# Second input projection as three float32r products by column group and half depth, with the embedding norm in two VectorE operations and the meta rows first

## The reference, cut to what matters

```python
x = x + (1.0 + gate[:, None, :]) * y            # end of the first block
x = rmsnorm(x, final_g)
...
meta = jnp.broadcast_to(meta_tokens...)         # 16 meta rows in front
h = _layernorm(jnp.concatenate([meta, x], axis=1), ln_emb_g, ln_emb_b)   # 528 rows
...
z = jnp.einsum('bld,dc->blc', h, w_in)          # [528,1024] x [1024,1472]
q_a, kv_a, k_pe, q_g, k_g, v_g = jnp.split(z, IN_OFFSETS, axis=-1)
# rmsnorm of parts of z, rotations, attention over 528 keys, w_o, layernorm,
# router, 32 experts with 4 per token, layernorm
```

## Time and profile before

| | |
|---|---|
| median of 3 runs | 2195.67 us (2194.2 to 2202.55) |
| profiled execution, its own time | 2200.66 us |
| its span in the trace | 2198.9 us |
| mean granted TensorE clock | 0.966 of full |
| PE busy | 2063.0 us (94%) |
| DVE busy | 1729.9 us (79%) |
| ACT busy | 1298.4 us (59%) |
| POOL busy | 289.6 us (13%) |

### The profile page before, as it was taken

The page is one execution under the profiler, slowest core; times in us unless marked ns, Lnnn a source line. Parts: engine busy times, 40 slices in busy tenths (PEclk is TensorE's granted clock), DMA queues, the critical chain, the costliest instruction groups (busy, mean ns, idle before and its releaser), DMA issues.

```text
span 2198.9 us, 28821 instructions
## 1 busy us (share of the span) xinstructions
PE 2063.0 (94%) x8636; PEld 1508.0 (69%) x8636; DVE 1729.9 (79%) x1915; ACT 1298.4 (59%) x1642; POOL 289.6 (13%) x251
## 2 busy tenths in 40 slices
PE   4997999897898999899999999999999999999994
PEld 2443444785444678688888888888888888888883
DVE  5799985435444446699999999999999999999996
ACT  1001664222223552487888888888887878878784
POOL 5000000000100001112121212121212121111110
PEclk7999999998999999699999999999999999999997
DMA  7211212521102005599999999999999999999994
GB/s 288 76 58 58 77 58 96 201 94 37 49 34 67 20 4 175 193 359 356 374 358 369 357 368 357 370 359 369 359 370 354 374 348 372 353 375 351 369 343 155
DMA packets 146522, 533.47 MB, mean 243 GB/s; under 512 B 11728, under 2 KB 17008, under 8 KB 142704
## 3 DMA queue, kind: packets, MB, share of 16 engines
q1 hardware_dynamic: 132912, 492.45, 60.9%
q0 software_dynamic: 13568, 40.48, 7.1%
HBM read 517.68 MB, written 25.17 MB: 247 GB/s over the span
## 4 chain that ended last, share of the span: by engine, by line
PE 82%; DVE 11%; ACT 3%; issue 2%; DMA 2%; POOL 0%; SPq 0%; DVEq 0%; ACTq 0%; POOLq 0%
PE ps L757 46%; PE ps L827 7%; DVE arena L1501 6%; PE ps L931 4%; PE ps L886 4%; PE ps L706 3%; PE ps L675 2%; PE ps L867 2%; PE ps L1034 2%; PE ps L780 1%; PE ps L700 1%; ACT arena L1421 1%; DVE arena L1987 1%; DVE arena L1981 1%; ACT arena L1419 1%
## 5 line engine op out<-in xcount | busy, mean ns | idle before, releaser
L757 PE MATMUL ps<-split,xTs 128*128 128x512 f32 x3264 | 779.5, 393 | 3.1 <-ACT split L1413 3.1
L757 PEld LDWEIGHTS ps<-split,xTs 128*128 128x128 f32 x3264 | 609.2, 188 | 129.6 <-ACT split L1413 3.5
L1968 DVE TENSOR_TENSOR split<-ring,split 128x2048 fp32r<-128x2048 f32 x204 | 465.8, 2288 | 24.1 <-ACT split L1413 23.2
L1413 ACT ACTIVATE split<-ring 128x1024 fp32r<-128x1024 f32 x408 | 411.1, 1058 | 120.0 <-PE ps L757 85.6
L1968 DVE TENSOR_TENSOR split<-arena,split 128x2048 fp32r<-128x2048 f32 x204 | 466.3, 2286 | 13.7 <-ACT split L1413 12.4
L1413 ACT ACTIVATE split<-arena 128x1024 fp32r<-128x1024 f32 x408 | 409.5, 1053 | 94.9 <-PE ps L757 94.9
L757 PE MATMUL ps<-split,aTs 128*128 128x512 f32 x1632 | 385.1, 391 | 0.0
L757 PEld LDWEIGHTS ps<-split,aTs 128*128 128x128 f32 x1632 | 303.9, 188 | 62.3
L827 PE MATMUL ps<-arena,ring 128*128 128x512 f32 x640 | 281.2, 599 | 11.0 <-DVE arena L1526 9.6
L827 PEld LDWEIGHTS ps<-arena,ring 128*128 128x128 f32 x640 | 122.8, 192 | 167.7 <-issue 166.7
L1501 DVE SCALAR_TENSOR_TENSOR arena<-arena,chan 128x512 f32<-128x512 f32 x240 | 180.3, 751 | 7.7
(11 more groups left out here) (343 smaller groups left out, 2009.5 us busy)
## 6 DMA issues: line engine op xcount, KB each, us to landing
ring<-in_w_gate_up SPq DMA_DIRECT2D x170, 1024.0 KB, 8.1
arena<-in_w_gate_up SPq DMA_DIRECT2D x102, 1024.0 KB, 6.2
arena<-in_w_down SPq DMA_DIRECT2D x102, 1024.0 KB, 10.3
ring<-in_w_down SPq DMA_DIRECT2D x34, 1024.0 KB, 10.4
ring<-in_w_in SPq DMA_DIRECT2D x24, 1024.0 KB, 4.8
ring<-in_mod_w SPq DMA_DIRECT2D x12, 1024.0 KB, 6.0
ring<-in_w_out SPq DMA_DIRECT2D x8, 1024.0 KB, 4.9
ring<-in_pw_w SPq DMA_DIRECT2D x4, 1024.0 KB, 5.4
```

The lines of the kernel that those rows point to most:

```text
L757: m = mm(ps[:, banks + q, :], lhs[:, x_, k, :], w[:, q * 512:(q + 1) * 512], start=start, stop=stop)
L1413: A(split[:, 0, c % SPLITS, :], chunk(c), ACT.Copy).then_inc(sig("hi_ready"), 1)
L1968: V.tensor_tensor(split[:, 1, s_, :].rearrange("p a b -> p (a b)"), chunk_pair(p), split[:, 0, s_, :].rearrange("p a b -> p (a b)"), ALU.s ...
```

## The change

The projection takes float32r halves of its weights and of its input; the ring tile is split by ScalarE and VectorE as the tiles before it are, and can be refilled from then on. A unit is done in two halves of the depth (`z_half`), 12 matmuls each, because `split` holds two tiles. VectorE writes the low part of the turned input (`h_low`). The meta rows are the first tile (`ORDER`) and are loaded from DRAM earlier. The bias add leaves GpSimd: `norm_apply` is now two operations with a tensor and a scalar each. TensorE, ScalarE and VectorE get new orders:

```diff
+        hz = [xTs, aTs, m2.take(2, KD, P, of=arena_r), m2.take(2, KD, P, of=arena_r), hTm]
+        ORDER = [TC] + list(range(TC))
+        Z_BANK = [1, 4, 5, 6, 7] + [4, 5, 6, 7] + [4, 5, 6, 7, 3]
+        Z_ENDS = (LC, LC + TC, 2 * LC + TC)
 last_use:
-            if n < T_IN2:
+            if n < T_Q:
                 return sig("w_lo"), n - T_PW2 + 1
-            if n < T_Q:
-                return sig("z_ready"), (LC, LC + TC, 2 * LC + TC)[(n - T_IN2) // 2]
 split_done (for tiles of this projection):
+            elif s % 2 == 0:
+                eng.wait_ge(sig("z_used"), (s - N_PW2 - N_OUT) // 2 + 1)
+            else:
+                eng.wait_ge(sig("z_ready"), Z_ENDS[(s - N_PW2 - N_OUT) // 2])
 GpSimd:
-            pool.wait_ge(sig("out_used"), N_OUT + TC - 1)
+            pool.wait_ge(sig("pw2_ready"), 2 * N_PW2)
             pool.dma_start(h[0:META, TC, :], a["meta_tokens_2"][:, :])
-            for t in range(LC): ... tensor_tensor(h, h, rows1[0:r, 2, :], ALU.add).then_inc(sig("h_ready"), 1)
 TensorE:
+            def turn_h(i):
+                if i >= 2:
+                    pe.wait_ge(sig("hT_lo"), 2 * (i - 1))
+                    pe.wait_ge(sig("z"), 1)
+            def z_half(unit, kk):
+                pe.wait_ge(sig("w_lo"), N_PW2 + N_OUT + n + 1)
+                if g == 0:
+                    pe.wait_ge(sig("hT_lo"), 2 * unit + 2)
+                elif kk == 0 and t < TC:
+                    pe.wait_ge(sig("z"), unit - 3)
+                for q in range(4):
+                    for x_, w_ in THREE:
+                        i = mm(ps[0:r, Z_BANK[unit], 0:wd], hz[t][:, x_, k, :], w[w_][:, q, :], ...)
+            turn_h(0)
+            turn_h(1)
+            z_half(0, 0)
+            z_half(1, 0)
+            z_half(0, 1)
+            z_half(1, 1)
+            for i in range(2, LC):
+                turn_h(i)
+                z_half(i, 0)
+                z_half(i, 1)
+            for t in range(TC):
+                z_half(LC + t, 0)
+                if t >= 2:
+                    turn_a(t - 2)
+            for t in range(TC):
+                z_half(LC + t, 1)
+                if t < 3:
+                    turn_a(t + 2)
+            for t in range(LC):
+                z_half(LC + TC + t, 0)
+                if t in (2, 4):
+                    turn_heads(t // 2 - 1, 4, rot[:, 0:512], 1, AT_B)
+            for t in range(LC):
+                z_half(LC + TC + t, 1)
+                if t < 2:
+                    turn_heads(t + 2, 4, rot[:, 0:512], 1, AT_B)
 ScalarE, in order: h_rstd(0), weights_high(W_Z), squares(0), h_rstd(1), h_out(0), h_out(1), squares(1),
   weights_high(W_Z + 1), h_rstd(2), z_out(0), h_out(2), z_out(1), squares(2), h_rstd(3), h_out(3), z_out(2),
   squares(3), h_rstd(4), h_out(4), z_out(3), weights_high(W_Z + 2), z_out(4), weights_high(W_Z + 3),
   z_rstd(0..4), a_out(0..4), weights_high(W_Z + 4), then z_out and z_rstd of the four units of B,
   weights_high(W_Z + 5), b_out(0), b_out(1), then z_out, b_out, z_rstd of C
 VectorE:
             def norm_apply(i):
+                st.link(V.scalar_tensor_tensor(h[0:r, t, :], h[0:r, t, :], bn_mv[0:r, t, 0:1], rows1[0:r, 1, :], ALU.subtract, ALU.mult))
+                dve.wait_ge(sig("emb_rstd"), i + 1)
+                V.scalar_tensor_tensor(h[0:r, t, :], h[0:r, t, :], emb_rstd[0:r, t:t + 1], rows1[0:r, 2, :], ALU.mult, ALU.add).then_inc(sig("h_ready"), 1)
   in order: norm_stats(TC), norm_apply(0), weights_low(W_Z), norm_stats(0), norm_apply(1), h_low(0), norm_stats(1),
   h_low(1), weights_low(W_Z + 1), norm_apply(2), norm_stats(2), h_low(2), norm_apply(3), norm_stats(3), h_low(3),
   norm_apply(4), z_sums(0), z_sums(1), h_low(4), z_sums(2), weights_low(W_Z + 2), z_sums(3), weights_low(W_Z + 3),
   z_sums(4), rotate_a(0..4), weights_low(W_Z + 4), z_sums of B, weights_low(W_Z + 5), rotate_heads of B, z_sums of C
   and rotate_heads of C
```

More of the change, by code:

```diff
@@ L328, in rows_of @@
             return P if t < TC else META
[L331 removed]
+        BANK_QN = [4 + j for j in range(HM)]
         ONE = cst("one")
@@ L1251, in _ @@
             nc.scalar.preload_act_table_set("natural_log_exp_and_others")
-            norm_h(0)
-            for t in range(LC):
-                if t + 1 < LC:
-                    norm_h(t + 1)
-                h_out(t)
-                if t >= 1:
-                    z_out(t - 1)
-            z_out(TC)
-            for t in range(LC):
-                z_rstd(t)
-            for t in range(LC):
-                if t < TC:
-                    z_out(LC + t)
-                a_out(t)
-                if t < TC:
-                    z_rstd(LC + t)
+            W_Z = N_PW2 + N_OUT
+            h_rstd(0)
+            weights_high(W_Z)
+            squares(0)
+            h_rstd(1)
+            h_out(0)
+            h_out(1)
+            squares(1)
+            weights_high(W_Z + 1)
+            h_rstd(2)
+            z_out(0)
+            h_out(2)
+            z_out(1)
+            squares(2)
+            h_rstd(3)
+            h_out(3)
+            z_out(2)
+            squares(3)
+            h_rstd(4)
+            h_out(4)
+            z_out(3)
+            weights_high(W_Z + 2)
+            z_out(4)
+            weights_high(W_Z + 3)
+            for i in range(LC):
+                z_rstd(i)
+            for i in range(LC):
+                a_out(i)
+            weights_high(W_Z + 4)
+            for t in range(TC):
+                z_out(LC + t)
+                z_rstd(LC + t)
+            weights_high(W_Z + 5)
+            b_out(0)
+            b_out(1)
             for t in range(LC):
                 z_out(LC + TC + t)
-                if t < TC:
-                    b_out(t)
+                if t < 2:
+                    b_out(t + 2)
                 z_rstd(LC + TC + t)
@@ L1666, in _ @@
             st.link(V.memset(z_ss, 1.0))
+            norm_stats(TC)
+            norm_apply(0)
+            weights_low(W_Z)
             norm_stats(0)
-            for t in range(LC):
-                if t + 1 < LC:
-                    norm_stats(t + 1)
-                norm_apply(t)
+            norm_apply(1)
+            h_low(0)
+            norm_stats(1)
+            h_low(1)
+            weights_low(W_Z + 1)
+            norm_apply(2)
+            norm_stats(2)
+            h_low(2)
+            norm_apply(3)
+            norm_stats(3)
+            h_low(3)
+            norm_apply(4)
             def z_sums(unit):
@@ L1754, in _ @@
                 dve.wait_ge(sig("rotated"), AT_C + t + 1)
+                if t == 0:
+                    z_sums(LC + TC + 3)
+                    z_sums(LC + TC + 4)
             for t in range(TC):
```

215 lines of the change are left out of this document (108 added, 107 removed).

## The result

The changed kernel takes 2183.66 us (2183.08 to 2184.66, 4 runs) against 2198.72 (2194.2 to 2202.55, 4 runs) for the kernel before in the same session: a ratio of 0.9933, 95% interval 0.9909 to 0.9956, so 15.1 us faster. The forecast was 2184.3. That the two agree to 0.6 us is partly luck. The kernel before came out 3.05 above the median that the forecast started from, and the gain was 15.1 where 11.4 was predicted. In the two profiled executions the difference is 2198.9 - 2182.9 = 16.0 us of span.

The account below looks back on a forecast made before the run. TensorE was taken to bound the kernel, with waits on a serial chain in group A. Groups A, B and C summed to an end at 648.8 instead of 660.16, 11.4 us gained: 2195.67 - 11.4 = 2184.3 us, range 2175 to 2193.

Parts of the forecast that it names:

- Group A: First projection group: a shorter serial chain and cheaper products end it at 576.35, where it ended at 585.60 before.
- serial blocks: In group A, tiles 1 and 2 each take 12.3 us: turn, 4.0 idle, product 4.9, slow stretch 2.4.
- I count one: In group A, one half-clock stretch, costing 2.4 us on average, after TensorE's first idle gap of 3.4 us.
- 1.5 shorter as a chain: Embedding norm merged into two VectorE operations without GpSimd's add: 0.5 us dearer on VectorE, chain 1.5 shorter.
- Group B: Second projection group: eight halves of 2.77 and five small turns, 24.3 us, from 578.15 to 602.5.
- Group C: Third projection group: weight split delays start to 605.3, TensorE stands 10 us at turn_heads(0), end 648.8 against 660.16 before.
- The gain is handed on whole: After group C, q and kv parts, attention and experts wait for nothing later than now and keep the 11.4 us.
- Rival 1: Clock stays up in group A's gaps of 3.4, 4.0 and 4.0: gain 18.6 us, 2177; chance 0.15.
- Rival 2: Some 25 engine crossings in A's blocks and C cost 0.3 us more each: gain 3, 2192; chance 0.2.
- Rival 3: Clock does not come back between gaps in A and C: 21 us more, 2205.3, slower; chance 0.08.
- if TensorE were all that counted: Cheaper products in all groups: 5 x 1.1 for A plus 9 x 1.33, 17.5 us gained.

Follow-up runs that it names:

- experiment 4: Changed kernel with ScalarE's sums of squares of tiles 2 and 3 moved ahead of h_out and z_out: 2180.46 us, ratio 0.9923.
- experiment 12: experiment 5, still all in three products, with the next tile's norm ahead of this tile's copy, low part and product in group A: 2161.66 us, ratio 0.9841.
- experiment 10: experiment 5 with group A as plain float32 products from the ring, turned input copied to SBUF in float32: 2187.25 us, ratio 0.9959.
- experiment 11: experiment 10 with ScalarE's norm one tile ahead and, on VectorE, B's second split one rotation later: 2153.83 us, ratio 0.9811.
- experiment 2: Changed kernel with the merged norm undone, GpSimd adding the bias again: 2184.11 us, ratio 0.9944.
- experiment 1: Kernel before with only the merged norm, two VectorE operations and no GpSimd add: 2193.62 us, ratio 0.9981.
- experiment 5: Changed kernel with the splits of C's first and second weight tiles moved forward in the ScalarE and VectorE queues: 2170.48 us, ratio 0.9888.
- experiment 3: Kernel before with merged norm, meta rows first and their DMA sooner, products left plain float32 from the ring: 2174.64 us, ratio 0.9898.
- experiment 6: Changed kernel with the reorderings of experiment 4 and experiment 5 together: 2167.08 us, ratio 0.9864.
- experiment 8: Changed kernel with the input-low by weight-high product left out in groups B and C, output less exact: 2172.76 us, ratio 0.9893.
- experiment 7: Changed kernel with unused filler matmuls, 15 ahead of tiles 1 and 2 in A and 32 ahead of turn_heads(0): 2180.04 us, ratio 0.9933.

## Why the prediction was right, and where it was off

**Group A, ends 576.35; measured 574.95.** The mechanism stands, with its numbers: a 448-wide matmul at 0.204 (twelve start 2.45 apart), serial blocks of 11.5 and 12.5 (543.15 to 554.62 to 567.09) for 12.3, gaps of 3.95 twice for 4.0, caused by the squares behind `h_out` and `z_out` as written. Experiments 4 and 12 show that cause on this form, 10 and 11 on the plain one. Wrong was the first slow stretch: "I count one" after 3.4 us of idleness; the gap was 3.12 and the clock stayed at 1.00, 2.4 us too many in the sum. That the end came out only 1.4 sooner is luck: tile 0's first half began 1.1 late (535.76 for 534.7) and the last tile took 7.8 for 7.35.

**The merge, "1.5 shorter as a chain".** Experiment 2 shows it off the path that sets the end: C ends 0.2 us later without it, and the medians differ by under 0.5. The gap of 3.1 hides it, since the low part waits behind `norm_stats(1)`. In the old order it is worth 4.2 (experiment 1), which the prediction, made for the new order, did not ask.

**Group B, 24.3 long, from 578.15 to 602.5; measured 24.5, from 576.86 to 601.34.** Right: the eight halves and their small turns took 24.5 us, as summed from 0.231. The figure of the Trainium skill for a lone warm matmul of 512 (TensorE: Matmul & The Clock Gate, Back-to-back issue gap: 216 ns) is not met in this form: two halves back to back start 2.73 us apart (579.72 to 582.45), 228 ns for each of twelve.

**Group C, first product 605.3, hole 10, end 648.8; measured 604.19, 8.56, 647.55.** Right in place and cause. Experiment 5 shows it: with the splits forward the stall, the hole and the slow stretch are gone, and C is 14 us shorter in the trace. That the hole came out 1.4 shorter than I said is four alternating units at 2.5 (604.05 to 606.55 to 609.06) for 2.7, and the rest of the queue.

**"The gain is handed on whole".** The q and kv parts took 31.74 in place of 33.19, as the clock's mean there was 0.95 and not 0.85. And from the first product of attention to the end the span was 1505.55 before and 1503.61 after, 1.9 less. In all three executions on the old program's later part (before, experiments 1 and 3) this stretch took 1505.0 to 1505.6, and in the eleven others, with the merged semaphores, 1499.7 to 1503.7. No run separates it, so its cause stays open. In that stretch PE has the same 6902 matmuls and is busy 1.65 us less (1452.10 and 1450.45), so most of the 1.9 is not waiting time. These terms, 1.25 in the projection, 1.45, and 1.9, make the 4.6 by which the span fell more than the 11.4.

**The rivals.** Rival 1, the clock stays up, held for one gap of A's three. Rival 2, hand-overs, did not come: the blocks were 11.5 and 12.5 for 12.3. Rival 3, the slower one, did not either: after each gap full speed came back in 3.4 to 4.9 us.

**What the prediction did not say.** It asked whether the change gains, and not what each part is worth. The runs answer that. The three-product form pays in B and C: 5.3 us in B (where the old hole of 1.8 went and a wait of 1.9 at the start came), and once the queues allow 10.7 in C, of which 6.2 are the old hole of 3.11 and what the half clock behind it cost (half of 6.16). In A it does not, in the orders that were tried: VectorE needs 7.06 us for the norm of a tile (520.62 to 527.67 to 534.73 in the trace of experiment 11) and a plain unit with its turn takes TensorE 6.9, so the two are in step, while the cheaper product needs 1.3 more of VectorE for a low part and leaves TensorE to wait. The 5 x 1.1 us counted for A in "if TensorE were all that counted" became a loss of 4.1 there, in the better of the two orders (experiments 11 and 12).

## What to carry to other kernels

A cheaper product that needs more of the engine that feeds it is to be weighed stage by stage: it paid in two groups and cost in the third, in one loop nest. Before a stage is made cheaper, look at what stands in the queue ahead of the operation that releases it: the order of two queues moved 33 us between experiments 10 and 11 and 14 in C, more than any change in the work. And a gain found alone need not be there beside another change: one gap can hide another, as with the merged norm, or the clock can give back elsewhere what was won.

## What the runs showed of the hardware

**The half clock after a gap is not a function of the gap.** The same wait of 3.1 us ahead of tile 0's half was followed by twelve matmuls at full speed (2.66 to 2.71) in six kernels and at half speed (4.23) in experiment 6. The wait of 1.9 ahead of B was followed by full speed in six kernels (in experiment 8 with eight matmuls), and by 4.60 for 3.02 in experiments 4 and 6. The products of the kv part, unchanged in all, took 1.02 us a pair in some places and 1.91 in others, at different places in different kernels. Executions of one kernel differ in it too: those of experiment 7 had mean clocks of 0.969 to 0.973 with spans from 2182.1 down to 2173.3. The Trainium skill (TensorE: Matmul & The Clock Gate, What's actually happening) says that the number of slow matmuls at the start of one kernel differs from run to run; these stretches lie in the middle of it, and with one trace of each kernel no run shows how they move from run to run. A wait of 1.5 to 3.5 us should be priced as a chance; after each of 3.95 and more in this seam a slow stretch came. Where A had no wait at all, in experiments 3 and 11, the clock was 1.00 throughout.

**Three slow stretches in the changed kernel lasted 3.36, 4.89 and 4.51 us**, which costs half of that, 2.1 on average; the forecast had 2.4 from the four before.
